# A mixing stage rewritten: heads paired in the partitions, 256-wide products, the token shift moved into the projection

## What is computed

```
xn   = rms_norm(h, norm1_gain)
proj = xn @ w_in                              # 1024 x 3840: 2048 retention columns, 1792 RWKV columns
f    = proj_rw + (prev_token(proj_rw) - proj_rw) * mu      # token_shift_lerp, 1792 columns
r, k, v = f[0:512], f[512:1024], f[1024:1536]; w_lo, a_lo, g_lo = the last 64 + 64 + 128
decay = exp(-exp(-softplus(-(w0 + tanh(w_lo) @ w_up)) - 0.5));  a = sigmoid(a0 + a_lo @ a_up);  g = sigmoid(g_lo) @ g_up
for each token (8 heads of 64 x 64 state):
    state = state * decay + (state @ a_vec) b_vec^T + v k^T
    y     = state @ r
y = (head_norm(y) + bonus) * g
retention: 4 heads of 128, chunked, rotary q and k, head_norm, silu gate
mixed = concat(ret, rw);  h = h + mixed @ w_out;  then a 32-expert layer, layer two's mixers and its FFN
```

## Time and profile before

| | us |
|---|---|
| profiled execution, its own time | 3472.32 |
| span from first to last instruction | 3470.6 |
| median of three runs (lowest, highest) | 3475.03 (3473.43, 3487.86) |
| load, norm and projection, until PE stops | 0 to 390.9 |
| mixing, first row of a turn to the last output copy | 422.8 to 1143.8 |
| of that, one turn | about 86 |
| PE busy over the whole span | 3018.0 |

### The profile page before, as it was taken

The page is one execution under the profiler, slowest core; times in us unless marked ns, Lnnn a source line. Parts: engine busy times, 40 slices in busy tenths (PEclk is TensorE's granted clock), DMA queues, the critical chain, the costliest instruction groups (busy, mean ns, idle before and its releaser), DMA issues. The chain is left out here.

```text
span 3470.6 us, 41293 instructions
## 1 busy us (share of the span) xinstructions
PE 3018.0 (87%) x15368; PEld 2511.0 (72%) x15369; DVE 1739.6 (50%) x2244; ACT 1340.9 (39%) x1891; POOL 469.1 (14%) x403
## 2 busy tenths in 40 slices
PE   5999589999999672999999459887988899998997
PEld 4888478888888552888888358665766688887886
DVE  4111155555564434999999541375663433333313
ACT  4111133444442212777777342334452333332212
POOL 0000134444443002000000100031000000000000
PEclk9999788888888876999999779999998899999999
DMA  4222401111110434999999421100021211110113
GB/s 186 91 91 91 155 22 35 41 40 34 41 39 7 158 125 157 395 409 409 405 409 406 184 69 31 30 17 2 1 110 43 56 48 48 48 48 27 46 49 133
DMA packets 164478, 410.93 MB, mean 118 GB/s; under 512 B 28249, under 2 KB 115337, under 8 KB 151049
## 3 DMA queue, kind: packets, MB, share of 16 engines
q1 hardware_dynamic: 140922, 339.59, 26.7%
q10 hardware_dynamic: 14080, 36.70, 2.7%
q0 software_dynamic: 9360, 33.04, 2.4%
HBM read 347.92 MB, written 61.39 MB: 118 GB/s over the span
## 5 line engine op out<-in xcount | busy, mean ns | idle before, releaser
L134 PE MATMUL psum<-part,ffn_up_w_high 128*128 128x512 f32 x704 | 277.3, 394 | 4.8 <-DVE ffn_up_w_low L129 4.8
L135 PE MATMUL psum<-low,ffn_up_w_high 128*128 128x512 f32 x704 | 278.3, 395 | 0.0
L136 PE MATMUL psum<-part,ffn_up_w_low 128*128 128x512 f32 x704 | 274.1, 389 | 0.0
L2976 DVE SCALAR_TENSOR_TENSOR ffn_up_acc<-psum,ffn_up_taps,ffn_up_acc 128x1023 f32<-128x1023 f32 x88 | 112.8, 1282 | 297.0 <-ACT ffn_up_acc L2940 291.1
L134 PE MATMUL psum<-part,expert_x_high 128*128 128x512 f32 x512 | 206.7, 404 | 2.9 <-issue 1.5
L134 PE MATMUL psum<-project_w_high,high 128*128 128x480 f32 x512 | 195.4, 382 | 10.5 <-DVE project_w_low L129 10.4
L136 PE MATMUL psum<-part,expert_x_low 128*128 128x512 f32 x512 | 203.6, 398 | 0.0
L136 PE MATMUL psum<-project_w_high,low 128*128 128x480 f32 x512 | 196.3, 383 | 0.0
L135 PE MATMUL psum<-project_w_low,high 128*128 128x480 f32 x512 | 195.4, 382 | 0.0
L2940 ACT ACTIVATE ffn_up_acc<-psum,ffn_up_taps 128x1024 f32<-128x1024 f32 x44 | 53.1, 1206 | 345.5 <-PE psum L136 345.5
L129 DVE TENSOR_TENSOR expert_down_low<-expert_down,expert_down_high 128x2048 fp32r<-128x2048 f32 x64 | 143.7, 2287 | 43.7 <-ACT expert_down_high L124 43.7
(11 more groups left out here) (561 smaller groups left out, 7433.6 us busy)
## 6 DMA issues: line engine op xcount, KB each, us to landing
expert_gate<-in_w_gate_dram SPq DMA_DIRECT2D x32, 2048.0 KB, 9.8
expert_up<-in_w_up_dram SPq DMA_DIRECT2D x32, 2048.0 KB, 9.7
expert_down<-in_w_down_dram SPq DMA_DIRECT2D x32, 2048.0 KB, 10.7
ffn_up_w<-in_ffn_w_up_dram SPq DMA_DIRECT2D x44, 512.0 KB, 3.8
y_rows<-expert_y ACTq DMA_DIRECT2D x32, 512.0 KB, 11.0
proj<-project_out ACTq DMA_DIRECT2D x8, 1920.0 KB, 12.8
project_w<-in_w_in_dram SPq DMA_DIRECT2D x7, 1920.0 KB, 11.8
ffn_down_w<-in_ffn_w_down_dram SPq DMA_DIRECT2D x44, 256.0 KB, 2.7
```

Source lines behind the costliest of these rows:

```text
L134: pe.matmul(out, left[0], right[0], start=start, stop=False)
L135: pe.matmul(out, left[0], right[1], start=False, stop=False)
L136: return pe.matmul(out, left[1], right[0], start=False, stop=stop)
L2976: v.scalar_tensor_tensor(out=acc[c][u][:, i:], in0=wide(psum, 4 * u + 2 * c, 2)[:, 0:S - i], scalar=taps[:, last_tap - i, ds(at, 1)], in1= ...
```

## The change

*Projection.* The columns are taken in another order and width: first four blocks of 448 (the 1792 RWKV columns), then four of 512 (retention). After each RWKV block SP copies the block one partition down into `prev` (three transfers, one for the rows of the same tile, one for the first row of tiles 1 to 7, one of zeros), DVE does three operations of 128 x 3584 elements (subtract, times `mu`, add), and only then does SP store the block. Stores are issued by SP instead of ACT. The block loops are unrolled. Load stage and mixing stage lose the zero row, `prev`, `mu`, POOL's two and DVE's one shift operation a tile. SP loads features, v and retention inputs of tile t+2 apart, each as soon as its buffer is free.

*Heads paired.* Two heads share the 128 partitions: `b_t`, `kt_t` and `ar_t` hold head 2n on partitions 0 to 63 and head 2n+1 on 64 to 127. So each tilde is transposed in 4 instead of 8 pieces. `ar_t` holds a and r side by side, and one product of 256 columns replaces two of 128: 16 products a tile instead of 32. Neighbouring products alternate between the two partition halves and write to neighbouring banks.

*State and output transposed.* q (the right-hand side) and y are now made feature-major in banks 2 and 3: `m0` is block diagonal with two heads in a block, so 4 products of 256 columns do the state's part of both; v times `akrk` does the other part (8 of 256 columns, 64 weight columns each, alternating output halves), u times `rb` finishes y (8 of 128 columns). q and y are then transposed back (4 each) and copied by ACT. m stays 16 products, outputs alternating between the halves.

*Solve.* Five full steps; the sixth works on 64x64 pieces only (only the upper right quarter of x_t changes there), without `ab_step`. DVE starts x_t directly from PSUM, ACT's copy `ab` comes after that. ACT copies x_n at every step.

*Order.* POOL does `rotate` after the sixth `ab_step` product instead of before the first. The next tile's low-rank products move to steps 0 and 1 (the g product to the end of the turn), sigmoids to step 1, exponentials to step 5 ahead of ACT's zs copies. ACT's root of the retention norm of tile t-1, and DVE's division by it, move from step 4 to the end of the turn. The squash (tanh, copy, sigmoid) of the tile after next moves to the end of ACT's turn.

The diff, cut to its core:

```diff
+            def load_prev(b):
+                u = b % 2
+                sp.dma_start(prev[1:P, :, :], out[u][0:P - 1, :, 0:width]).then_inc(prev_loaded, 16)
+                sp.dma_start(prev[0:1, 1:TT, :], out[u][P - 1:P, 0:TT - 1, 0:width]).then_inc(prev_loaded, 16)
+                sp.dma_start(prev[0:1, 0, :], zeros[0:1, 0:width]).then_inc(prev_loaded, 16)
...
+                if b < RW_BLOCKS:
+                    load_prev(b)
+                if b + 2 < N:
+                    load(b + 2)
+                if b < RW_BLOCKS:
+                    sp.wait_ge(shifted, b + 1)
+                    to = rw_dram[:, b * width:(b + 1) * width]
+                else:
+                    to = ret_dram[:, blocks[b][0]:blocks[b][0] + RET_W]
+                sp.dma_start(to.rearrange("(t p) n -> p t n", p=P), cols(out[b % 2], b)).then_inc(stored[b % 2], 16)
...
+            def shift(b):
+                out_cols = cols(out[b % 2], b)
+                v.wait_ge(prev_loaded, (b + 1) * 48)
+                v.tensor_tensor(prev[:], prev[:], out_cols, ALU.subtract).then_inc(shift_order, 1)
+                v.wait_ge(mu_loaded, 16)
+                v.wait_ge(shift_order, b * 2 + 1)
+                v.tensor_tensor(prev[:], prev[:], per_block(mu[:, b * width:(b + 1) * width], TT), ALU.mult).then_inc(shift_order, 1)
+                v.wait_ge(shift_order, b * 2 + 2)
+                v.tensor_tensor(out_cols, out_cols, prev[:], ALU.add).then_inc(shifted, 1)
...
-        tilde_t = [st.sb(f"tilde_t_{n}", [RW_N, RW_HEADS, P]) for n in "bark"]
+        b_t, k_t_ = st.sb("b_t", [P, PAIR, P]), st.sb("kt_t", [P, PAIR, P])
+        ar_t = st.sb("ar_t", [P, PAIR, 2, P])
...
-                v.wait_ge(shift_order, t * 2 + 2)
-                v.tensor_tensor(feat[u][:], feat[u][:], prev[:], ALU.add).then_inc(shifted, 1)
-                v.wait_ge(shifted, t + 1)
...
+                for gr in range(2):
+                    v.wait_ge(b_scored, t * 2 + gr + 1)
+                    v.tensor_tensor(x_t[gr][:], two_banks(4 * gr)[:, :, 0, :], per_block(pair_mask[0][:], HG), ALU.mult)\
+                        .then_inc(x_started, 1)
+                    v.wait_ge(x_started, t * 2 + gr + 1)
+                    v.tensor_tensor(x_t[gr][:], x_t[gr][:], per_block(ident[:], HG), ALU.add).then_inc(x_ready, 1)
...
+                    to = x_t[gr][FIRST_HALF, :, SECOND_HALF]
+                    by = three(step_bank(s, gr)[FIRST_HALF, 0:HG * RW_N], HG)
...
+                if not first:
+                    ret_divide(t - 1, ret_link)
+                if not last:
+                    tildes(*after)
...
-            def shift(j, u):
-                t = 2 * j + u
-                pool.wait_ge(feat_ready[u], j * 16 + 16)
-                pool.wait_ge(prev_ready, t * 16 + 16)
-                pool.tensor_tensor(prev[:], prev[:], feat[u][:], ALU.subtract).then_inc(shift_order, 1)
-                pool.wait_ge(shift_order, t * 2 + 1)
-                pool.tensor_tensor(prev[:], prev[:], mu[:], ALU.mult).then_inc(shift_order, 1)
...
-                rotate(j, u, first)
...
+                        rotate(j, u, first)
...
+                    if s == 5 and not last:
+                        decays(*after)
...
                 if not first:
+                    ret_deviation(t - 1)
                     act.wait_ge(ret_ready, t)
...
+                act.wait_ge(y_turned, t + 1)
+                act.activation(y_raw[:], bank[0][:], ACT.Copy).then_inc(y_copied, 1)
+                if not last:
+                    take_g(*after, first)
+                if not (isinstance(j, int) and j == PAIRS - 1):
+                    squash(j + 1, u)
...
+            def products(left, b, done):
+                gr = b // 4
                 for h in range(HG):
                     hh = HG * gr + h
-                    last = pe.matmul(bank[4 * gr + at][:, h * P:(h + 1) * P], left[:, hh, :], right[:, hh, :],
+                    out = bank[b + h % 2][:, (h // 2) * 2 * P:(h // 2 + 1) * 2 * P]
+                    last = pe.matmul(out, left[side(hh), hh // 2, :], ar_t[side(hh), hh // 2, :, :].rearrange("p c s -> p (c s)"),
                                      start=True, stop=True)
-                last.then_inc(scored, 1)
+                last.then_inc(done, 1)
...
+            def raise_state(t):
+                pe.wait_ge(m0_ready, 2 * t + 2)
+                pe.wait_ge(k_masked[0], t + 1)
+                for n in range(PAIR):
+                    pe.matmul(bank[2 + n // 2][:, (n % 2) * 2 * P:(n % 2 + 1) * 2 * P], m0[:, n, :],
+                              ar_t[:, n, :, :].rearrange("p c s -> p (c s)"), start=(n % 2 == 0), stop=False,
+                              skip_group_check=True)
...
+                for h in range(HG):
+                    hh = HG * gr + h
+                    n = hh // 2
+                    last = pe.matmul(bank[2 + n // 2][side(hh), (n % 2) * 2 * P:(n % 2 + 1) * 2 * P], head(v_(u), hh, RW_N),
+                                     akrk[gr][:, slot(hh), :, :].rearrange("p c s -> p (c s)"), start=False, stop=False,
+                                     skip_group_check=True)
...
-                    to = head(bank[0], h, RW_N)
-                    pe.matmul(to, r_t[:, h, :], head(m0, h, RW_N), start=True, stop=False)
-                    pe.matmul(to, rb[h // HG][:, h % HG, :], head(u_, h, RW_N), start=False, stop=False)
-                    last = pe.matmul(to, rk[h // HG][:, h % HG, :], head(v_(u), h, RW_N), start=False, stop=True)
+                    n = h // 2
+                    out = bank[2 + n // 2][side(h), (n % 2) * 2 * P + P:(n % 2 + 1) * 2 * P]
+                    last = pe.matmul(out, head(u_, h, RW_N), rb[h // HG][:, slot(h), :], start=False, stop=True, skip_group_check=True)
...
+                pe.wait_ge(y_fm_ready, t + 1)
+                turn_heads(0, lambda h: y_fm[:, h, :], PAIR, y_turned)
+                if not last_turn:
+                    lift(2, *after)
```

More of the change, by code:

```diff
@@ L389, in _ @@
             for c in range(PIECES):
-                sp.dma_start(piece(w[0], c), w_dram[c * D // PIECES:(c + 1) * D // PIECES, 0:width]
+                sp.dma_start(piece(w[0], c), w_dram[c * D // PIECES:(c + 1) * D // PIECES, blocks[0][0]:blocks[0][0] + width]
                              .rearrange("(k p) n -> p k n", p=P)).then_inc(piece_loaded[c], 16)
-            load(0, 1)
-            with sp.Fori(1, half) as j:
-                for u in range(2):
-                    sp.wait_ge(odd_out, j * 8 + u * 4)
-                    load(j, u)
+            load(1)
@@ L927, in turn @@
                                            ALU.mult).then_inc(ab_split, 1)
-                    if s == 1 and not last:
-                        shift(j + u, 1 - u)
+                    if s == 2:
+                        rotate(j, u, first)
                 if not first:
@@ L1182, in turn, with turn_heads @@
+            def turn_heads(b, of, n_heads, done):
+                for h in range(n_heads):
+                    last = pe.transpose(bank[b][:, h * P:(h + 1) * P], of(h), ident[:])
+                last.then_inc(done, 1)
             def turn(j, u, first, last_turn):
```

772 lines of the change are left out of this document (409 added, 363 removed).

## The result

The changed kernel takes 3650.43 us (median of four runs, 3644.03 to 3656.69) against 3476.32 us: ratio 1.0494, 95% interval 1.0464 to 1.0524. I had forecast 3394 and a range of 3320 to 3455. The profiled execution took 3649.3 us, its span is 3647.1.

| us | before | after | difference |
|---|---|---|---|
| start to the last product of the projection | 390.9 | 682.7 | +291.8 |
| from there to the first low-rank transpose (428.3, 712.0) | 37.4 | 29.3 | -8.1 |
| from there to the first output product (1159.6, 1332.3) | 731.3 | 620.3 | -111.0 |
| the rest | 2311.0 | 2314.8 | +3.8 |

A forecast was written before the change was run, and what follows sets the result against it. PE was taken to bound the mixing stage, about a third of it at low clock. Eight turns save 78 us and the front 3, the projection 0: 3472.3 - 81 = 3391, median 3394 us, range 3320 to 3455.

The forecast's parts named there:

- The projection's copy: Projection: shift's transfers and three DVE operations take 26 to 40 us a block, beside 42 us of PE work.
- rival D: Projection: PE waits for `project_w_low` or banks, up to 3 x 10 us; 3424 us; chance counted within the forecast's 0.55.
- Linear width in the projection: Projection: blocks of 448 and 512 columns cost what 480 did; between +8 and -8 us, taken as 0.
- The mixing stage: Mixing: a turn falls from 86.8 to 77.1 us, 9.7 less, over eight turns 78 us.
- the front: Start of the mixing stage: loses the first tile's shift, DVE's addition alone 2.4 us; taken as 3.
- step 0: First solve step: 13.4 to 11.4 us, the clock staying low for a part; bounds 8.5 and 14.
- steps 3 and 4: Solve: step 3 grows from 7.6 to 9.8 us with decay sums, state's part and v's half; step 4 stays at 7.7.
- step 5: Last solve step: 6.8 to 6.3 us; PE's work halves, but ACT's zs copies stand behind table load and exponentials, 3.1.
- The end of the turn: End of a mixing turn: a chain over engines instead of PE's work, 30.6 to 27.4 us, bounds 22 and 32.
- Rival A: Mixing: clock stays up and neighbouring products pair; turn 67 us, kernel 3320 to 3302 us; chance 0.20.
- Rival B: Mixing: ACT's and DVE's chain grows, low clock lasts through step 2; turn 83 us, kernel 3444 us; chance 0.12.
- Rival C: Mixing: alternating partition or output halves costs 0.115 us a change (3461 us) or 0.25 (3540 us); chance 0.13.

The follow-up runs named there:

- a3: Changed kernel with the 127-partition copy into `prev` issued as two transfers, of 126 partitions and 1 partition: 3351.75 us.
- a1: Changed kernel with the 127-partition copy into `prev` issued as two transfers, of 112 and 15 partitions: 3356.37 us, ratio to before 0.9652.
- c1: a1 with pt and qd made early, exponentials moved a step earlier and the squash moved to the solve's first step: 3273.66 us, ratio to before 0.9438.
- b1: a1 with DVE making pt before the tildes and POOL making qd before the finished retention rows: 3311.68 us.
- b2: a1 with the three exponentials moved from the solve's last step to the end of the step before: 3318.96 us.
- b6: a1 with the products with b ordered as four on partitions 0 to 63, then four on 64 to 127: 3374.41 us.
- a5: Changed kernel with slow copy kept, SP issuing the weights of block b+2 before the copy, DVE's order unchanged: 3596.46 us.
- d2: Changed kernel copying partitions 1 to 127 to the same partitions, leaving out the shift for all but each tile's first token: 3580.57 us.

## Where the prediction failed, and where it held

- **The projection's copy: the step that failed.** I took 12.8 us for 1920 KB from the store of 128 partitions, at most doubled it, and called 26 to 40 us the bounds for the transfers and DVE's three operations together. From the issue to DVE's start alone it was 96, to the end of the three operations 108. The rows that I had can't price this copy, because none of them is a transfer of 127 partitions. With the right number the working stood: PE would wait for `project_w_low`, as rival D said, not up to 10 us three times, but 72 four times. The range was wrong because D's price was bounded by a row of another form.
- **A stated rule was passed over.** The Trainium skill's page DMA: Bandwidth & Descriptors, in the section named under a3, has the case of 127 partitions, and my prediction drew only on the page on tiling. An estimate from that rule and the store of the earlier trace rows, with one engine for sixteen, is 16 x 12.8 x 1778/1920 = 190 us. That is twice the 96 measured, but it would have put the whole forecast on the other side.
- **Linear width in the projection: right.** With the copy mended it ends at 388.3 (a1) and 384 (a3) against 390.9.
- **The mixing stage: right way, too small.** 77.1 forecast, 74.5 measured in turn 2, 72.5 in the mean. I counted 9.7 us for each turn; the first distance shrank by 21.6, the last by 15.4, the five between by 11.6 in the mean, and the stretch before the first transposes by 8.1 where I had 3 for the front. Mis-sized terms: step 0 has no low clock at all (8.5 instead of 11.4), steps 3 and 4 came out 2.2 shorter with the overlap in them, and step 5 took 9.9 for 6.3, because PE's wait for the exponentials and the low clock behind it were not priced, only ACT's copies.
- **The prices of the products.** The sum had the 16 products with b and k at 6.9 us, one after the other; at 2.00 for eight they take 4.0. It had v's eight at 3.4; at 1.01 for four they take 2.0. The sentence that products with 64 columns cost the same is wrong for 64 weight columns: m's took 0.12 each before already and 0.06 in c1, a gain of 1.0 us that the sum has at nothing. Two slips of adding are in it too: 22.3 + 5 is 27.3, and step 3's 9.8 is not the sum of its terms (7.6 + 1.8 + 1.7 is 11.1 without v's half), since what leaves the step has no price there; 8.8 was measured.
- **The end of the turn:** 26.7 for 27.4 in turn 2 (32.6 in the turn with the pause), and with the wait for pt that I had named. I had not asked whether that order was needed: b1 took the wait away.
- **Rival A** was half right: the overlap came, the clock did not stay up (0.87 in the stage). **Rival B**'s turn of 83 did not come, though the exponentials that it names were on the path (b2). **Rival C** is wrong: alternating halves costs nothing, it is what makes the overlap (b6).
- **The median** is 174 us above before, where the traces say 176.5: 292 lost in the projection less what the other stages gained. The 292 are the copy's, as a1 shows by getting back 294.

## What to carry to other kernels

Before pricing a transfer by another's bandwidth, compare the number in its outermost dimension: 127 partitions went over one DMA engine at 20 GB/s, the same rows as 112 + 15 or 126 + 1 went over fourteen to sixteen. A copy of 127 partitions, as a shift by one partition makes it, wants to be split. If it can't be, loads that others wait for want to be issued ahead of it (a5, 54 us less, though mostly by a shorter copy). In a stage whose engine drops its clock after waiting, price a wait at what it takes and, beside it, at what the work behind it takes at the lower clock: b2's 2.4 us of waiting were worth 5.6 a turn.

## What the runs showed of the hardware that I had not expected

- A transfer of 127 partitions keeps the issuing queue too: SP needed 84 us to issue the next small one, and the weights stood behind it.
- On one engine the pace depends on offset and order: 96 us as changed, 81 with a load issued just before (a5), 79 without the offset of one partition (d2). Why stays open.
- fp32 products of 256 columns cost 0.43 us in one form and 0.24 where neighbours lie on different halves of the input or of the output partitions; two and two overlap nearly as well (2.07 for eight) as one and one (2.00), four and four do not (2.94). Products of 64 moving columns cost 0.12 with 64 weight columns and 0.065 where these alternate the output half.
